# Retention in 64-token blocks on quarters of the TensorE array, with the key rotation, one DMA pair and two weight loads moved

## Chip, cores and metric

One NeuronCore of one Trainium2 chip runs the whole kernel. The metric is the device time in microseconds of one execution; a time of a kernel is the median of its runs. The profile is one such execution, and its times count from the first instruction (the span).

## What is computed

The reference is one layer of a streaming encoder for a prompt of 4096 tokens and a sample of 64 tokens, with model width 1024, all in fp32:

```python
h = _rmsnorm(x, norm_g) * (1.0 + scale) + shift
rq, rk, rv, rg, aq, ak, av, ag = _in_proj(h, w_in)      # one matmul, columns split
rq = _rope(rq, pos); rk = _rope(rk, pos) * RET_DK ** -0.5
r_out, state = _retention(rq, rk, rv)                   # 4 heads of 128
r_out = _head_norm(r_out) * jax.nn.silu(rg)
a_out = sliding_window_attention_with_sinks(aq, ak, av) * jax.nn.silu(ag)
x = x + gate * (concatenate([r_out, a_out]) @ w_out)
y = _rmsnorm(x, final_g)

def _retention_chunk(R, q, k, v):                       # one block of L tokens
    s = einsum('bqhd,bkhd->bhqk', q, k) * decay         # decay[i, j] = g**(i - j), 0 above the diagonal
    out = einsum('bhqk,bkhv->bqhv', s, v) + einsum('bqhd,bhdv->bqhv', q, R) * g**(i + 1)
    R = g**L * R + einsum('bkhd,bkhv->bhdv', k * g**(L - 1 - j), v)
```

The block length L is free as far as the result goes. The reference uses 64.

## The kernel before

Tokens go in tiles of 128: 32 tiles of the prompt (t = 0 to 31) and one (t = 32) that holds the sample in its upper half. The program has two phases, each a loop over tiles, and every engine has its own instruction list with waits on semaphores. SP issues all DMAs, in the order of its list.

Phase A (`slot`, t = 0 to 33) makes the four retention projections of tile t and the retention of tile t-1. The projections are split matmuls: activations and weights are each cut into a high and a low fp32r part, and three products of 8 matmuls of 512 columns are added (`dense`, L1298, the matmul itself L1305), so 24 matmuls for each of the groups q, k, v and gate. TensorE's order in a slot is: q projection into bank `za0`; the retention block of the tile before; k projection into `za1`; v into `za0`; gate into `za1`. A bank is written again only when VectorE or ScalarE have read it (`zq_read`, `zk_read`, `v_done`, `rg_done`).

The retention block (L1384 to L1404) is plain fp32 and works on the whole tile of 128 tokens: per head a 128x128 score matmul (L1389), a state update `k_row` x `v_dec` (L1395), and two matmuls into the bank `out_b`, the queries on the state (L1401) and the decayed scores on the values (L1403).

VectorE's list in a slot (L949 to L1057): transpose the keys (L958), scale the next tile's x (L913), decay the scores (L964), rotate the queries out of `za0` (L942, L944, L947), group norm statistics of `out_b` (L983), state update (L992), aggregate (L996), transpose the next tile's x (`turn_x`, L919), normalise `out_b` into `r_out` (L1005) and gate it (L1010), rotate the keys out of `za1` (L942 to L947 again), transpose and scale the queries (L1024, L1026), split the next tile's h into its parts (`split_h`, L926 and L928), decay the values (L1041), finish the gate (L1047). ScalarE modulates x into h between `turn_x` and `split_h` (L726), copies the values (L762) and takes the tanh of the gate (L774). GpSimd takes the powers for the two norms.

SP's list in a slot: store the scaled x (L445) and load it back in blocks of 32 rows for the transpose (L430), the same for the rotated queries (L461), store h (L469), load the next rope table (L471), store the retention output (L477), then the store and four loads of the rotated keys (L481, L430). The weights of the attention projections and of the output come in pieces of 1 MB through four staging buffers (`load_piece`, L290), are rounded by ScalarE (`split_hi`, L317) and their low part made by VectorE (`split_lo`, L321). At slot 4 TensorE also computes the output gate of adaLN (L1458), VectorE adds its bias (L1056), and SP stores it and then loads two weight pieces (L493 to L499).

Phase B (`slot_b`) does the attention and the output projection. Its matmuls for the attention use parts of the array: L1501 is stationary 128x64 (half the columns), L1508 is 64x64 (a quarter), L1478 is 64x128 (half the rows). A `tile_position` gives the rows and columns of the array.

Of the kernel before, what the change touches and what calls it, by code (L numbers as in the profile page):

```python
# [31 lines left out]
F32 = mybir.dt.float32  # L32
# [27 lines left out]
def build_program(nc, x_prompt, x_sample, c_prompt, c_sample, state_ret, cache_k, cache_v, norm_g, w_ada,  # L60
# [5 lines left out]
    with ctx:  # L66
# [14 lines left out]
        small = sb("small", [P, 64])  # L81
# [32 lines left out]
        decay = sb("decay", [P, COLS], F32, phase_a)  # L114
        qdec = sb("qdec", [P, COLS], F32, phase_a)
        tiny_a = sb("tiny_a", [P, 176], F32, phase_a)
# [3 lines left out]
        c_in = tiny_a[:, 36:52].rearrange("p (c k) -> p c k", c=2)  # L120
        c_th = tiny_a[:, 52:68].rearrange("p (c k) -> p c k", c=2)
        c_silu = tiny_a[:, 68:84].rearrange("p (k c) -> p k c", c=2)
        g_col = tiny_a[:, 84:92]
        h_scale = tiny_a[:, 108:124].rearrange("p (k c) -> p k c", c=2)
        h_shift = tiny_a[:, 124:140].rearrange("p (k c) -> p k c", c=2)
# [76 lines left out]
        state_out, wide_set = sem("state_out"), sem("wide_set")  # L202
# [182 lines left out]
        def ag_bank(i, t):  # L385

            return out0_b if static(i) and t == 0 else kg_b

        def static(i):
            return isinstance(i, int)  # L390

# [7 lines left out]
        def _(sp):  # L399
# [34 lines left out]
            def slot(i, u):  # L434
# [43 lines left out]
                if not pe_turns(i, t) and (not static(i) or t < SAMPLE):  # L478

                    wait(sp, k_done, t + 1)  # L480
                    sp.dma_start(k_dram[t], k_row[:, :]).then_inc(k_stored, 16)  # L481
                    wait(sp, k_stored, 16 * t)
                    wait(sp, x_turned, t)
                    load_blocks(k_in, k_dram[t], k_loaded)
# [8 lines left out]
                if static(i) and t == 4:  # L493
                    sp.wait_ge(gate_rows, 1)
# [3 lines left out]
                    for n in range(B_KV, B_Q + 1):  # L498
                        load_piece(sp, n)  # L499
# [398 lines left out]
        def _(dve):  # L898
# [50 lines left out]
            def slot(i, u):  # L949
# [11 lines left out]
                if back:  # L961
                    wait(dve, s_ready, t)
                    wait(dve, out_ready, t - 1)
                    V.tensor_tensor(s_t[:, :], qs_b[:, :], decay[:, :], ALU.mult).then_inc(st_done, 1)  # L964
                if front:
# [4 lines left out]
                    rotate(t, za0, q_row, zq_read, q_mul, q_done)  # L970
                if static(i) and t == SAMPLE:
# [7 lines left out]
                if back:  # L979
                    wait(dve, out_ready, t)  # L980
                    wait(dve, gn_mv_done, t - 1)
                    for h in range(RH):
                        last = V.bn_stats(gn_stats[:, h, :], out_b[:, h * DK:(h + 1) * DK])  # L983
# [4 lines left out]
                    wait(dve, upd_ready, t)  # L988
                    st = state_s if static(i) and t - 1 == SAMPLE else state
                    for h in range(RH):  # L990
                        cols = slice(h * DK, (h + 1) * DK)
                        last = V.scalar_tensor_tensor(st[:, cols], st[:, cols], GAMMA[h] ** P, upd_b[:, cols], ALU.mult, ALU.add)  # L992
# [5 lines left out]
                if more and not (static(i) and t == 0):  # L998
                    turn_x(*nxt)
                if back:  # L1000
                    wait(dve, gn_rstd_done, t)
                    wait(dve, yr_stored, 16 * (t - 1))
                    for h in range(RH):
                        cols = slice(h * DK, (h + 1) * DK)
                        last = V.tensor_scalar(r_out[:, cols], out_b[:, cols], gn_mv[:, h, 0:1], gn_rstd[:, h:h + 1],  # L1005
# [616 lines left out]
```

## Time and profile before

| | |
|---|---|
| median of 3 runs | 1841.93 us (1838.59 to 1841.97) |
| profiled execution | 1841.76 us |
| its span | 1840.0 us |
| TensorE matmul busy | 97% of the span |
| VectorE, ScalarE, GpSimd busy | 63%, 31%, 6% |
| mean granted TensorE clock | 0.991 |
| DMA | 296.64 MB, 161 GB/s over the span |

Phase A ends and phase B begins at about 886 us. An engine's busy share is an average over both phases and over the start and the change of phase; which engine sets the time has to be read in each. In a timeline row the first number is the start, the second the time from the start of the row's first instruction to the end of its last; the ends of matmuls are modelled, so the distance of starts is the better measure.

### The profile page before, as it was taken

What the parts mean: (1) busy time and instruction counts of PE and PEld (TensorE: products, weight loads), DVE (VectorE), ACT (ScalarE), POOL (GpSimd) and SP (SyncE); (2) the same over time, 40 slices, a digit from 0 to 9 for tenths busy, and PEclk for the clock granted to TensorE, in tenths of its full rate; (3) what the DMA queues carried; (4) which work ended last, traced back from release to release, by engine and by line L of the source; (5) the groups of instructions that cost most, each with busy time, mean ns of one, the idle gap of its engine ahead of it and who ended that gap; (6) DMA issues with size and microseconds to landing.
All of it is one profiled execution on the core that took longest, in us unless ns stands there. A gap on an engine that the chain in (4) does not pass through costs nothing.

```text
span 1840.0 us, 31120 instructions
## 1 busy us (share of the span) xinstructions
PE 1790.7 (97%) x9668; PEld 1482.1 (81%) x9668; DVE 1159.3 (63%) x2590; ACT 579.2 (31%) x2032; POOL 116.7 (6%) x278
## 2 busy tenths in 40 slices
PE   5999999999999999999799999999999999999997
PEld 2788788888888888888678888888888888888885
DVE  3665666655666555666756766766666666666666
ACT  3321222212222212222434434434434344344342
POOL 1000000000000000000000000000000000000000
PEclk8999999999999999999899999999999999999999
DMA  9666555555555554554666565575565665665655
GB/s 372 200 170 181 143 130 148 137 137 140 129 148 147 126 146 133 134 141 132 200 172 163 150 190 148 157 190 143 160 187 142 170 172 146 182 166 145 188 145 139
DMA packets 488481, 296.64 MB, mean 161 GB/s; under 512 B 348634, under 2 KB 423594, under 8 KB 487412
## 3 DMA queue, kind: packets, MB, share of 16 engines
q1 hardware_dynamic: 488436, 296.08, 58.5%
q8 instruction: 24, 0.39, 0.1%
q14 instruction: 21, 0.17, 0.0%
HBM read 174.27 MB, written 121.71 MB: 161 GB/s over the span
## 4 chain that ended last, share of the span: by engine, by line
PE 89%; issue 3%; DVE 3%; DMA 2%; SPq 1%; ACT 1%; POOL 0%; POOLq 0%; DVEq 0%; ACTq 0%
PE bank L1305 78%; PE bank L1478 3%; PE bank L1501 2%; PE bank L1403 2%; PE bank L1401 2%; PE bank L1395 2%; PE bank L1389 2%; PE bank L1508 1%; DVE wl L321 1%; DMA xn_scratch<-xn 1%; DMA xp<-xn_scratch 0%; DMA stage<-in_w_out 0%; SPq L517 0%; SPq L430 0%; DMA xt<-in_x_prompt 0%
## 5 line engine op out<-in xcount | busy, mean ns | idle before, releaser
L1305 PE MATMUL bank<-wh,hh 128*128 128x512 f32 x1584 | 399.6, 394 | 7.5 <-DVE hh L1085 2.7
L1305 PE MATMUL bank<-wl,hh 128*128 128x512 f32 x1584 | 391.9, 389 | 0.6 <-DVE wl L321 0.6
L1305 PE MATMUL bank<-wh,hl 128*128 128x512 f32 x1584 | 392.5, 390 | 0.0
L1305 PEld LDWEIGHTS bank<-wh,hh 128*128 128x128 f32 x1584 | 293.6, 189 | 69.0 <-issue 8.0
L1305 PEld LDWEIGHTS bank<-wl,hh 128*128 128x128 f32 x1584 | 297.5, 188 | 62.9 <-DVE wl L321 1.1
L1305 PEld LDWEIGHTS bank<-wh,hl 128*128 128x128 f32 x1584 | 297.9, 188 | 61.9
L726 ACT ACTIVATE hf<-xn,tiny_a 128x128 f32<-128x128 f32 (+1 forms) x248 | 98.6, 480 | 368.2 <-DVE xn L919 368.2
L1228 DVE SCALAR_TENSOR_TENSOR a_gate<-a_gate,bank 128x128 f32<-128x128 f32 x132 | 29.1, 282 | 174.9 <-ACT a_gate L875 174.9
L1305 PE MATMUL bank<-wh,yh 128*128 128x512 f32 x528 | 132.7, 393 | 0.0
L1305 PE MATMUL bank<-wh,yl 128*128 128x512 f32 x528 | 130.9, 389 | 0.0
L1305 PE MATMUL bank<-wl,yh 128*128 128x512 f32 x528 | 130.8, 389 | 0.0
L802 ACT ACTIVATE p_in<-bank,tiny_b 128x128 f32<-128x128 f32 x264 | 108.3, 410 | 33.6 <-DVE tiny_b L1123 33.6
L1305 PEld LDWEIGHTS bank<-wh,yh 128*128 128x128 f32 x528 | 100.0, 190 | 21.3 <-DVE yl L1159 0.4
L1305 PEld LDWEIGHTS bank<-wl,yh 128*128 128x128 f32 x528 | 99.3, 188 | 20.7
L1305 PEld LDWEIGHTS bank<-wh,yl 128*128 128x128 f32 x528 | 99.0, 188 | 20.7
L1047 DVE SCALAR_TENSOR_TENSOR r_gate<-r_gate,bank 128x512 f32<-128x512 f32 x33 | 22.7, 688 | 134.9 <-ACT r_gate L774 134.9
L805 ACT ACTIVATE p_in<-bank,tiny_b 128x64 f32<-128x64 f32 x264 | 95.4, 361 | 0.0
L964 DVE TENSOR_TENSOR s_t<-bank,decay 128x512 f32<-128x512 f32 x33 | 22.8, 692 | 97.3 <-PE bank L1389 97.3
L1117 DVE TENSOR_REDUCE tiny_b<-bank 128x2 f32<-128x384 f32 x132 | 67.7, 553 | 5.3
L875 ACT ACTIVATE a_gate<-bank 128x256 f32<-128x256 f32 x66 | 21.7, 381 | 156.2 <-PE bank L1305 156.2
L762 ACT ACTIVATE v_row<-bank 128x512 f32<-128x512 f32 x33 | 19.8, 599 | 153.8 <-DVE v_dec L1041 153.8
L805 ACT ACTIVATION_READ_ACCUMULATOR p_in<-bank,tiny_b 128x1 f32 x264 | 67.4, 255 | 0.0
(167 smaller groups left out, 2430.0 us busy)
## 6 DMA issues: line engine op xcount, KB each, us to landing
xt<-in_x_prompt SPq DMA_DIRECT2D x64, 512.0 KB, 4.0
p_scratch<-p_in SPq DMA_DIRECT2D x264, 96.0 KB, 1.8
p_in<-p_scratch SPq DMA_DIRECT2D x66, 384.0 KB, 3.4
h_scratch<-hf SPq DMA_DIRECT2D x33, 512.0 KB, 2.9
hf<-h_scratch SPq DMA_DIRECT2D x33, 512.0 KB, 4.9
out<-xt SPq DMA_DIRECT2D x32, 512.0 KB, 4.4
xn_scratch<-xn SPq DMA_DIRECT2D x31, 512.0 KB, 2.9
xp<-xn_scratch SPq DMA_DIRECT2D x124, 128.0 KB, 3.0
```

The source lines that it names most:

```text
L726: last = nc.scalar.activation(hf[:, k, lo:P], src, ACT.Identity, bias=h_shift[:, k, c:c + 1], scale=h_scale[:, k, c:c + 1])
L802: nc.scalar.activation(p_out[:, :, g, 2 * c, :], scores_g[:, whole:whole + P].rearrange("p (b c) -> p b c", b=4), ACT.Exp, bias=s_bias[:, ...
L805: nc.scalar.activation(p_out[:, 2 * c:2 * c + 2, g, 1, :], scores_g[:, part:part + HALF].rearrange("p (b c) -> p b c", b=2), ACT.Exp, bias ...
L1117: last = V.tensor_reduce(s_max[:, m:m + 2], s_banks[2 * half + g][:, 0:6 * HALF].rearrange("p (c k) -> p c k", c=2), mybir.AxisListType.X, ...
L1228: last = V.scalar_tensor_tensor(ag, ag, 1.0, z, ALU.add, ALU.mult)
L1305: ins = mm(out, a[:, k, :], b[:, k, :], start=first and n == part[0] and k == chunks[0], stop=last and n == part[-1] and k == chunks[-1])
L1389: last = mm(qs_b[:, c], k_t[:, c], q_t[:, c], start=True, stop=True)
L1395: last = mm(upd_b[:, c], k_row[:, c], v_dec[:, c], start=True, stop=True)
L1401: mm(out_b[:, c], q_t[:, c], st[:, c], start=True, stop=False)
L1403: last = mm(out_b[:, c], s_t[:, c], v_row[:, c], start=False, stop=True)
L1478: last = mm(s_banks[2 * half + g][:, c * 3 * HALF:(c + 1) * 3 * HALF], q[rows, 2 * half + c, :], window(k, rows, u, c), start=n == 0, stop ...
L1501: mm(weighed(i, t, c)[cols, :], v[:, cols], p_t[:, :, g, 2 * c, :], start=True, stop=False, tile_position=(0, g * HD))
```

## The change

The retention works in blocks of 64 tokens: two per tile, c = 0 and c = 1, on parts of the array that do not overlap.

- The scores of the two blocks are two matmuls of 64 moving columns per head, on the two column halves of the array. The cross part of the 128x128 scores is not computed.
- The state update of each block is a matmul over 64 rows, on the two row halves, into two banks (`upd_b`, `ky_b`). VectorE makes a state after the first block, `state_mid`, in addition to the state after the second.
- The queries of block 0 meet `state`, those of block 1 `state_mid`, on the two column halves; the decayed scores of 64x64 meet the values on quarters of the array. The odd heads put block 0 in the lower and block 1 in the upper rows of the output bank, and go to `xb0` instead of `out_b`.
- The matmuls that make the output (`weighted_values`) come behind the k projection in TensorE's list. In the last slot, which has no projection, they follow the update at once.
- VectorE rotates the keys, and transposes the next x, ahead of the group norm. It normalises and gates the output behind the split of h, at the slot's end. Odd heads are normalised in two halves.
- SP stores and loads the rotated keys ahead of the store of h, the rope load and the store of the output.
- At slot 4 SP loads one of the two weight pieces before it waits for the gate's rows; the rows and the other piece come at slot 5.

```diff
+        state_mid = sb("state_mid", [P, COLS], F32, phase_a)
@@ SP, slot(i, u)
+                if not pe_turns(i, t) and (not static(i) or t < SAMPLE):
+                    wait(sp, k_done, t + 1)
+                    sp.dma_start(k_dram[t], k_row[:, :]).then_inc(k_stored, 16)
+                    wait(sp, k_stored, 16 * t)
+                    wait(sp, x_turned, t)
+                    load_blocks(k_in, k_dram[t], k_loaded)
                 if not static(i) or t + 1 <= SAMPLE:
                     wait(sp, h_done, t + 2)
...
                     wait(sp, yr_done, t)
                     sp.dma_start(yr_dram[t - 1], r_out[:, :]).then_inc(yr_stored, 16)
-                if not pe_turns(i, t) and (not static(i) or t < SAMPLE):
...
                 if static(i) and t == 4:
+                    load_piece(sp, B_Q)
+                if static(i) and t == 5:
                     sp.wait_ge(gate_rows, 1)
...
-                    for n in range(B_KV, B_Q + 1):
-                        load_piece(sp, n)
+                    load_piece(sp, B_KV)
@@ VectorE, slot(i, u)
-                    V.tensor_tensor(s_t[:, :], qs_b[:, :], decay[:, :], ALU.mult).then_inc(st_done, 1)
+                    V.tensor_tensor(s_t[:, 0:RH * HALF], qs_b[:, 0:RH * HALF], decay[:, :], ALU.mult).then_inc(st_done, 1)
                 if front:
...
                     rotate(t, za0, q_row, zq_read, q_mul, q_done)
+                if back:
+                    wait(dve, upd_ready, t)
+                    wait(dve, out_ready, t - 1)
+                    wait(dve, state_done, t - 1)
+                    for h in range(RH):
+                        last = V.scalar_tensor_tensor(state_mid[:, cols], st[:, cols], GAMMA[h] ** HALF, upd_b[:, cols],
+                                                      ALU.mult, ALU.add)
+                    last.then_inc(mid_done, 1)
...
+                if front:
+                    wait(dve, za_ready, 4 * t + 2)
+                    rotate(t, za1, k_row, zk_read, k_mul, k_done)
+                if more and not (static(i) and t == 0):
+                    turn_x(*nxt)
+                if back:
+                    wait(dve, out_ready, t)
+                        last = V.bn_stats(gn_stats[:, h, :], out_of(h))
+                        last = V.scalar_tensor_tensor(st[:, cols], state_mid[:, cols], GAMMA[h] ** HALF, ky_b[:, cols],
+                                                      ALU.mult, ALU.add)
+                    last.then_inc(state_done, 1)
+                        last = V.bn_aggr(gn_mv[:, h, :], gn_stats[:, h, :])
...
                     V.tensor_tensor(heads(v_dec[:, :]), heads(za0[:, :]), vdec..., ALU.mult).then_inc(vdec_done, 1)
+                if more:
+                    split_h(*nxt)
+                if back:
+                    wait(dve, gn_rstd_done, t)
+                        if row_block(h, 0) == 0:
+                            last = V.tensor_scalar(r_out[:, cols], out_of(h), ...)
+                        else:
+                            for c in range(2):
+                                last = V.tensor_scalar(r_out[c * HALF:(c + 1) * HALF, cols], out_of(h)[at, :], ...)
+                    V.scalar_tensor_tensor(r_out[:, :], r_out[:, :], 0.5, r_gate[:, :], ALU.mult, ALU.mult).then_inc(yr_done, 1)
+                if front:
                     if static(i) and t == SAMPLE:
                         for n in range(B_GATE, B_OUT):
                             split_lo(dve, n)
@@ TensorE
+            def weighted_values(i, t):
+                wait(pe, gn_done, t - 1)
+                wait(pe, mid_done, t)
+                for h in range(RH):
+                    for c in range(2):
+                        cols, at = slice(h * DK, (h + 1) * DK), row_block(h, c)    # row_block: HALF * ((c + h) % 2)
+                        if h == RH - 1 and c == 1:
+                            wait(pe, st_done, t)
+                        mm(out_of(h)[at:at + HALF, :], q_t[:, h * DK + c * HALF:h * DK + (c + 1) * HALF],
+                           (st, state_mid)[c][:, cols], start=h < 2, stop=False, tile_position=(0, at))
+                for h in range(RH):
+                    for c in range(2):
+                        last = mm(out_of(h)[at:at + HALF, :], s_t[rows, h * HALF:(h + 1) * HALF], v_row[rows, cols],
+                                  start=False, stop=h >= 2, tile_position=(c * HALF, at))
+                last.then_inc(out_ready, 1)
...
                     for h in range(RH):
-                        last = mm(qs_b[:, c], k_t[:, c], q_t[:, c], start=True, stop=True)
+                        for c in range(2):
+                            last = mm(qs_b[c * HALF:(c + 1) * HALF, h * HALF:(h + 1) * HALF], k_t[:, tok], q_t[:, tok],
+                                      start=True, stop=True, tile_position=(0, c * HALF))
...
-                        last = mm(upd_b[:, c], k_row[:, c], v_dec[:, c], start=True, stop=True)
+                        for c in range(2):
+                            last = mm((upd_b, ky_b)[c][:, cols], k_row[rows, cols], v_dec[rows, cols], start=True, stop=True,
+                                      tile_position=(c * HALF, 0))
                     last.then_inc(upd_ready, 1)
-                    for h in range(RH):
-                        mm(out_b[:, c], q_t[:, c], st[:, c], start=True, stop=False)
-                        last = mm(out_b[:, c], s_t[:, c], v_row[:, c], start=False, stop=True)
+                    if not front:
+                        weighted_values(i, t)
...
                         dense(za1[:, :], h_hi, h_lo, group(1)).then_inc(za_ready, 1)
+                    if back:
+                        weighted_values(i, t)
```

Smaller edits follow from these: the gate's rows of slot 4 go to the free half of `qs_b`, one bank of phase B's first tile is another one, and the decay tables are made for 64 tokens.

## Rows read from the trace of the kernel before

**Rows 1.** The page: the chain that ended last, by engine.

```profile
PE 89%; issue 3%; DVE 3%; DMA 2%; SPq 1%; ACT 1%; POOL 0%; POOLq 0%; DVEq 0%; ACTq 0%
```

**Rows 2.** Timeline of TensorE over one slot of phase A (start, duration, instruction).

```profile
535.19 2.07 PE L1305 MATMUL bank<-wh,hh 128*128 128x512 f32 x8
537.11 1.98 PE L1305 MATMUL bank<-wl,hh 128*128 128x512 f32 x8
...
555.24 1.98 PE L1305 MATMUL bank<-wh,hl 128*128 128x512 f32 x8
557.05 1.05 PE L1389 MATMUL bank<-q_t,k_t 128*128 128x128 f32 x8
...
560.54 2.07 PE L1305 MATMUL bank<-wh,hh 128*128 128x512 f32 x8
```

**Rows 3.** Slot of phase A: length; PE, PEld, DVE, ACT, POOL busy; clock; DMA.

```profile
532.50:557.80 25.30, 25.30 (x130) 21.55 (x129) 15.63 (x33) 5.43 (x12) 1.96 (x4) 1.00 0.53 136
```

**Rows 4.** Timeline of TensorE over the attention of one slot of phase B.

```profile
1128.94 1.98 PE L1305 MATMUL bank<-wh,yl 128*128 128x512 f32 x8
1130.85 0.65 PE L1501 MATMUL bank<-s_row,v_prev 128*64 128x256 f32 x4
...
1131.86 0.43 PE L1508 MATMUL bank<-s_row,v_row 64*64 64x256 f32 x1
...
1132.13 0.38 PE L1508 MATMUL bank<-s_row,v_row 64*64 64x256 f32 x1
...
1132.46 0.36 PE L1478 MATMUL bank<-ak_h,aq_h 64*128 64x192 f32 x2
1132.65 0.27 PE L1478 MATMUL bank<-ak_l,aq_h 64*128 64x192 f32 x2
...
1133.76 0.28 PE L1478 MATMUL bank<-ak_h,aq_l 64*128 64x192 f32 x2
1133.97 1.22 PE L1305 MATMUL bank<-wkvh,hh 128*128 128x256 f32 x8
1135.03 1.12 PE L1305 MATMUL bank<-wkvl,hh 128*128 128x256 f32 x8
1135.99 1.12 PE L1305 MATMUL bank<-wkvh,hl 128*128 128x256 f32 x8
```

**Rows 5.** Timeline of VectorE and ScalarE over the same slot.

```profile
536.40 0.88 DVE L992 SCALAR_TENSOR_TENSOR state<-state,bank 128x128 f32<-128x128 f32 x4
...
538.43 1.25 DVE L919 STREAM_TRANSPOSE xn<-xp 128x1024 f32<-128x1024 f32 x1 [0.85 <-DMA xp<-xn_scratch]
539.60 1.33 DVE L1005 TENSOR_SCALAR r_out<-bank,tiny_a,small 128x128 f32<-128x128 f32 x4
...
539.85 3.19 ACT L726 ACTIVATE hf<-xn,tiny_a 128x128 f32<-128x128 f32 x8 [11.75 <-DVE xn L919]
```

**Rows 6.** Slot 5: the chain's longest DMA, then timeline rows of VectorE and TensorE.

```profile
170.97 8.49 DMA xn_scratch<-xn
...
185.12 1.25 DVE L919 STREAM_TRANSPOSE xn<-xp 128x1024 f32<-128x1024 f32 x1 [6.84 <-DMA xp<-xn_scratch]
...
172.41 1.05 PE L1389 MATMUL bank<-q_t,k_t 128*128 128x128 f32 x8
...
189.59 3.63 PE L1305 MATMUL bank<-wh,hh 128*128 128x512 f32 x8 [2.56 <-DVE k_row L944]
...
202.20 1.05 PE L1389 MATMUL bank<-q_t,k_t 128*128 128x128 f32 x8
```

**Rows 7.** Slot 1: timeline of TensorE at its first projection.

```profile
61.65 2.08 PE L1305 MATMUL bank<-wh,hh 128*128 128x512 f32 x8 [0.77 <-ACT v_row L762]
```

**Rows 8.** Slots 32 and 33: timeline of VectorE, then of TensorE.

```profile
878.54 4.48 DVE L321 TENSOR_TENSOR wl<-stage,wh 128x2048 fp32r<-128x2048 f32 x2
883.57 0.69 DVE L1047 SCALAR_TENSOR_TENSOR r_gate<-r_gate,bank 128x512 f32<-128x512 f32 x1 [0.55 <-ACT r_gate L774]
...
884.52 0.39 PE L1401 MATMUL bank<-state_s,q_t 128*128 128x128 f32 x2
```

More of the change, by code:

```diff
@@ L80, in build_program @@
         ident = sb("ident", [P, P])
-        small = sb("small", [P, 64])
+        small = sb("small", [P, 32])
         neg_half = small[:, 0:8]
@@ L385, in ag_bank, with row_block, out_of @@
         def ag_bank(i, t):
-            return out0_b if static(i) and t == 0 else kg_b
+            return out1_b if static(i) and t == 0 else kg_b
         def static(i):
             return isinstance(i, int)
+        def row_block(h, c):
+            return HALF * ((c + h) % 2)
+        def out_of(h):
+            return (out_b, xb0)[h % 2][:, h * DK:(h + 1) * DK]
         def pe_turns(i, t):
@@ L978, in slot @@
                         split_lo(dve, n)
-                if back:
-                    wait(dve, out_ready, t)
-                    wait(dve, gn_mv_done, t - 1)
-                    for h in range(RH):
-                        last = V.bn_stats(gn_stats[:, h, :], out_b[:, h * DK:(h + 1) * DK])
-                    last.then_inc(gn_stat_done, 1)
-                    wait(dve, gn_stat_done, t)
-                    wait(dve, gn_var_done, t - 1)
[L988 to L992, printed above, removed]
-                    last.then_inc(state_done, 1)
-                    for h in range(RH):
-                        last = V.bn_aggr(gn_mv[:, h, :], gn_stats[:, h, :])
-                    last.then_inc(gn_mv_done, 1)
[L998 to L1005, printed above, removed]
-                                               ALU.subtract, ALU.mult)
-                    last.then_inc(gn_done, 1)
-                    wait(dve, gn_done, t)
-                    wait(dve, rg_done, t)
-                    V.scalar_tensor_tensor(r_out[:, :], r_out[:, :], 0.5, r_gate[:, :], ALU.mult, ALU.mult).then_inc(yr_done, 1)
                 if front:
@@ L1031, in slot @@
                     split_lo(dve, B_KV)
-                if more:
-                    split_h(*nxt)
                 if static(i) and t == 0:
@@ L1366, in dense_kv @@
                 dense(kg_b[:, 0:KV], *h_of(i, t), (wkvh, wkvl)).then_inc(zb_ready, 1)
+            def weighted_values(i, t):
+                wait(pe, gn_done, t - 1)
+                wait(pe, mid_done, t)
+                st = state_s if static(i) and t - 1 == SAMPLE else state
+                for h in range(RH):
+                    for c in range(2):
[4 more added lines that the diff above has]
+                           (st, state_mid)[c][:, cols], start=h < 2, stop=False, tile_position=(0, at))
+                for h in range(RH):
+                    for c in range(2):
+                        rows, cols = slice(c * HALF, (c + 1) * HALF), slice(h * DK, (h + 1) * DK)
+                        at = row_block(h, c)
+                        last = mm(out_of(h)[at:at + HALF, :], s_t[rows, h * HALF:(h + 1) * HALF], v_row[rows, cols],
+                                  start=False, stop=h >= 2, tile_position=(c * HALF, at))
+                last.then_inc(out_ready, 1)
             def slot(i, u):
@@ L1443, in slot @@
                         wait(pe, k_done, t + 1)
+                        wait(pe, state_done, t)
                         for h in range(RH):
@@ L1486, in weigh @@
                 t = 2 * i + u
+                if static(i) and t == 0:
+                    pe.wait_ge(gn_done, SAMPLE + 1)
                 if static(i) and t == SAMPLE:
```

65 lines of the change are left out of this document (38 added, 27 removed).

## The prediction

> **What bounds the kernel now.** I read the page's chain first: 89% of it is TensorE [rows 1]. Then the timeline of TensorE in one slot of phase A. The distance between the first projections of two slots is 25.35 us (535.19 to 560.54). Ten rows of 8 projection matmuls take 18.13 us (537.11 to 555.24), 1.813 us a row, so the twelve rows of a slot take 21.76 us and 3.59 us are left for the retention block. The scores begin at 557.05, exactly one row after 555.24 [rows 2]. So in a steady slot TensorE never waits, and the block's 3.59 us are on the path in each of the 33 slots that have one. The block has 16 fp32 matmuls, recorded as two passes each: 32 passes of 128 columns, 0.112 us each. VectorE is busy 15.63 of 25.3 us of such a slot [rows 3]. Nothing but TensorE's own time, and the places where it does wait, can move the result.
>
> **The retention block.** After the change it has 32 matmuls, 64 passes, and all run on parts of the array. Phase B already works so, and its timeline gives both sides of the trade [rows 4].
>
> The gain: on quarters (L1508) four passes start together, at 1131.86 and again at 1132.13. On row halves (L1478) a pair starts every 0.111 us (1132.65 to 1133.76 is ten steps). On column halves (L1501) 8 passes of 256 columns take 1.01 us to the start of L1508; one after the other they would take 8 x 0.22 = 1.8 us, at 0.112 us for 128 columns. So halves do run two at a time and quarters four.
>
> The cost: each change of shape. Without one, the row at 1128.94 would end at 1130.75; L1501 begins at 1130.85, a gap of 0.10. L1501 needs 4 x 0.22 = 0.88 of its 1.01 us, so its own slow first step and the gap to L1508 cost 0.13 together. L1508's first step is 0.27 instead of 0.22, and L1478 comes 0.33 after the second, a gap of 0.11. L1478's first step is 0.19 instead of 0.11. From its last pair to the full array are 0.21 instead of 0.11, and the first full row takes 1.06 us (1133.97 to 1135.03) where the next takes 0.96. By kind: into column halves or quarters 0.10 + 0.05 = 0.15 us, into row halves 0.11 + 0.08 = 0.19, back to the full array 0.10 + 0.10 = 0.20.
>
> The sum for the new block, in its order:
> - Scores on column halves: 16 passes of 64 columns, 8 steps. No row has so short a pass. If time goes with columns it is 0.056 a step, 0.45 us; if a step has a floor at what the pairs of L1478 need, 0.111, it is 0.89 us. I take 0.46: on row halves the floor was there with 128 stationary columns, and here both operands have 64.
> - Update on row halves: 16 passes of 128 columns, 8 steps, 0.89 us.
> - Queries on the states, column halves: 8 steps, 0.89 us.
> - Scores on values, quarters: 4 steps, 0.45 us.
> - Six changes: into column halves 0.15, into row halves 0.19, to the full array 0.20 (the k projection), into column halves 0.15, into quarters 0.15, to the full array 0.20: 1.04 us. The update's first step may cost 0.11 instead of 0.08, as its passes are longer than those of L1478; I take 1.07.
>
> That is 2.69 + 1.07 = 3.76 us against 3.59: **0.17 us more in each slot**. What the array gains by packing (0.9 us) the six changes take back. Over the 32 slots that have projections: +5.4 us. Bounds: with the gaps alone (six of 0.10) the block is 3.29, 0.30 less; with the score floor and 0.22 for each change 4.44, 0.85 more: -9.6 to +27.2 us.
>
> The Trainium skill, TensorEngine Tiling (Array Packing), section Theoretical Speedup, allows up to 2x for one small dimension and up to 4x in 64x64 tiles. Taken alone it leaves the 2.69 us of streams and 29 us gained in 32 slots; the trace agrees with the factors, but not with that sum, because it shows the changes between them.
>
> **What hides the rest of a steady slot.** I lay the slot out from the q projection's start, with 1.81 us a row and 0.2 us from one engine to the next. TensorE: q to 5.4, scores and update to 7.3, k to 12.8, output matmuls to 14.4, v to 20, gate to 25.5.
> - VectorE's `state_mid` is four instructions like the state update, 0.88 us [rows 5]. It comes after the query rotation, from 8.8 to 9.7. TensorE needs it at 12.8: 3 us of cover. If that went, each microsecond over it would cost 32 us.
> - Two more half-size normalisations cost two of L1005's, 1.33 / 4 each, so 0.67 us [rows 5]; the score decay on half the columns saves at most 0.3. VectorE goes from 15.6 to about 16.9 of 25.5 us: nothing on the path.
> - Key rotation: 13.0 to 15.1 (from the k projection's end), read by the gate projection at 20: 5 us of cover. `turn_x` then takes 1.25 us to 16.3; before it stood at 12.2, and 0.85 us of that was a wait for its DMA [rows 5], which now has 3 us of room. ScalarE's modulation, 3.19 us [rows 5], ends at 19.6. `split_h` follows the v projection and `v_dec`, 21 to 22.8; the next q projection needs it at 25.5: 2.7 us of cover.
> - The output's normalisation and gate end at 25.5, the gate's end and the key transpose at 27.9, needed by the next scores at 30.9: 3 us.
> - SP: the key store and its four loads now come at 15 to 21, ahead of the h store (h ready at 19.6) and the rope load, which nobody needs before the next slot; the output's store is last, at 25.6, before the next slot's x store. GpSimd's power for the group norm is asked for at 18.4 and used at 22.8. Cost zero, by these covers.
>
> **Slot 5.** Before, two pieces of 1 MB go out ahead of slot 5's x store, which takes 8.49 us. `turn_x` waits 6.84 us for it, the key rotation stands behind `turn_x`, and TensorE stops at 189.59 and then runs its next 8 matmuls in 3.63 us, twice the usual. From scores to scores the slot takes 29.79 instead of 25.35 us (172.41 to 202.20) [rows 6]: 4.44 us lost. After, one piece is asked for before the x store and the key rotation no longer stands behind `turn_x`. Both would be enough: with a DMA as late as before `turn_x` ends 3 us later than planned and `split_h` still within the slot. **-4.4 us.** Bounds: 0 to -4.4.
>
> **Start.** At slot 1 TensorE waits 0.77 us for the copy of the values [rows 7], which waits for VectorE behind the split of h and the scaling of the sample's state. With `v_dec` ahead of the split the copy is hidden and the split ends last: -0.5 us (0 to -0.8). At slot 30 the order costs about as much, 0.2, since the split of a weight piece now stands ahead of `v_dec` and of `split_h` with it.
>
> **Slots 32 and 33.** Here VectorE is the late one. Before, it normalises the output of slot 32 while TensorE works, splits two weight pieces from 878.54 for 4.48 us, finishes the gate at 883.57, and slot 33's output matmuls start at 884.52 [rows 8]. Now the normalisation (1.33 + 0.67) and its gate (0.69, an instruction like L1047) stand behind `v_dec`, ahead of the weight pieces: 2.7 us in the queue that were hidden before, less about 1 us in which VectorE waited for the v projection. Then come the gate's end, the score decay, and 0.88 us of `state_mid`, for which slot 33's output matmuls wait with nothing else to do. They start about 2.4 us later. What follows in phase B's start hangs on TensorE and on VectorE's next weight pieces, so it moves along: **+2.4 us** (0 to 3.5). Phase B itself is as before.
>
> **Sum.** +5.4 - 4.4 - 0.5 + 0.2 + 2.4 = +3.1 us on the profiled execution's 1841.76 us, 0.17 below the median: about **1845 us**.
>
> **Rivals.**
> - *The changes of shape are mostly hidden* (faster). If the weight load of the new shape overlaps the last passes of the old, the gaps alone are left and the block is 3.29: 1841.8 - 9.6 - 2.3 = 1830 us. For it: nothing in the old block shows a gap. Against it: all four changes in phase B show gap and slow first step in one sum. It decides once the six changes cost less than 0.85 us (block under 3.55, at which the total is 0.2% under). Chance 0.18.
> - *Short passes have a floor, or the passes of odd and even heads do not pair.* Scores at 0.111 a step: +0.43 a slot, 14 us more, 1859. In `weighted_values` the halves follow as A B B A, where phase B has A B A B; if each second pair went one after the other the state part would take 1.34 instead of 0.89, again 14 us. Against it: two passes per matmul already pair across halves. Chance 0.2.
> - *Slot 5 keeps its stall*, the pieces at slots 4 and 5 each delaying an x store: 1849. Chance 0.08.
> - The forecast as summed: 0.54.
>
> **Numbers.** A difference of 0.2%, 3.7 us, is about what a measurement of this kernel can tell from none. The forecast's own range, 1840 to 1850, crosses the upper bound of that (1845.6): of its 0.54 some 0.34 are within 0.2% and 0.2 slower. With the rivals: faster 0.18, same 0.34, slower 0.48. The 80% range reaches half way to the fast rival and nearly to the floor: 1835 to 1858.
>
> **What would show it.** Per slot: scores to scores 25.5 us, six short gaps in TensorE, scores row under 0.6 us, no wait of TensorE for `state_mid`. Slot 5 as long as slot 6. Slot 33: TensorE waits for `state_mid` for 2 us. I am wrong if the distance of slots is under 25.3 (changes cheaper) or over 25.8 (floor or broken pairs), or if TensorE waits for VectorE in steady slots.

## The result and the profile after

The kernel after takes **1864.55 us** (median of 4 runs, 1863.7 to 1866.37), the kernel before 1841.76. The ratio is 1.0128, interval 1.0116 to 1.014: slower by 1.3%. The forecast was 1845, its range 1835 to 1858; the result lies above the range. The profiled execution took 1863.72 us with a span of 1861.6, so it is 21.65 us longer than the span before, of 1839.96.

The chain on the page, by engine, says that the bound is still TensorE [rows 1]:

```profile
PE 91%; issue 3%; DVE 2%; DMA 2%; ACT 1%; POOL 1%; SPq 0%; POOLq 0%; DVEq 0%; ACTq 0%
```

The timeline of TensorE over one slot of phase A, after (start, duration, instruction), answers to [rows 2]:

```profile
534.54 0.69 PE L1438 MATMUL bank<-q_t,k_t 128*64 128x64 f32 x16
535.16 1.16 PE L1446 MATMUL bank<-v_dec,k_row 64*128 64x128 f32 x16
536.25 2.13 PE L1333 MATMUL bank<-wh,hh 128*128 128x512 f32 x8
538.22 2.02 PE L1333 MATMUL bank<-wl,hh 128*128 128x512 f32 x8
540.08 2.02 PE L1333 MATMUL bank<-wh,hl 128*128 128x512 f32 x8
542.03 0.32 PE L1406 MATMUL bank<-state,q_t 128*64 128x128 f32 x1
...
543.06 0.67 PE L1412 MATMUL bank<-v_row,s_t 64*64 64x128 f32 x16
543.65 2.13 PE L1333 MATMUL bank<-wh,hh 128*128 128x512 f32 x8
545.62 2.02 PE L1333 MATMUL bank<-wl,hh 128*128 128x512 f32 x8
547.48 2.02 PE L1333 MATMUL bank<-wh,hl 128*128 128x512 f32 x8
...
556.75 1.98 PE L1333 MATMUL bank<-wl,hh 128*128 128x512 f32 x8
558.56 1.98 PE L1333 MATMUL bank<-wh,hl 128*128 128x512 f32 x8
560.47 0.69 PE L1438 MATMUL bank<-q_t,k_t 128*64 128x64 f32 x16
```

The block stands in two pieces, as planned, and TensorE never waits. But look at the projections, whose code the change doesn't touch. From 538.22 to 540.08 and from 545.62 to 547.48 a row of 8 takes 1.86 us, where [rows 2] have 1.81. The rows from 556.75 on take 1.81. The first nine rows of this slot multiply `hh1` and `hl1`, the last three, the next tile's queries, `hh0` and `hl0`. So slots alternate: 25.93 us with nine rows of `hh1` and `hl1`, 25.71 with three; the mean is 25.82, against 25.35 before.

Phase B, which the change leaves alone but for banks, has the same. The timeline of its output projection after, and a slot of phase A and one of phase B in the windows view (length; PE, PEld, DVE, ACT, POOL busy; clock; DMA):

```profile
1134.91 2.03 PE L1333 MATMUL bank<-wh,yh 128*128 128x512 f32 x8
1136.78 2.02 PE L1333 MATMUL bank<-wl,yh 128*128 128x512 f32 x8
1138.64 2.02 PE L1333 MATMUL bank<-wh,yl 128*128 128x512 f32 x8
...
534.54:560.47 25.93, 25.93 (x162) 20.71 (x161) 17.20 (x39) 5.43 (x12) 1.96 (x4) 1.00 0.52 134
1120.00:1148.26 28.26, 28.26 (x164) 22.94 (x164) 18.20 (x46) 11.07 (x50) 1.34 (x5) 1.00 0.57 162
```

Rows on `yh` and `yl` take 1.86 us too. Before they took 1.81: this row starts so much ahead of the first one of [rows 4], at 1128.94:

```profile
1127.13 1.98 PE L1305 MATMUL bank<-wl,yh 128*128 128x512 f32 x8
```

Rows on `hh0` stay at 1.81; a slot of phase B takes 28.26 instead of 27.98 us. The granted clock is 1.00, the upper of its two levels (2.4 GHz), in the slots of both phases, as in [rows 3], so the clock is not the cause.

The other places that the prediction named, after: slot 1's first projection, the scores of slots 5 and 6, then TensorE's waits at slots 31 and 33 and what VectorE does ahead of the second (in brackets the idle time before an instruction and what ended it):

```profile
60.31 2.13 PE L1333 MATMUL bank<-wh,hh 128*128 128x512 f32 x8
...
173.09 0.69 PE L1438 MATMUL bank<-q_t,k_t 128*64 128x64 f32 x16
198.99 0.69 PE L1438 MATMUL bank<-q_t,k_t 128*64 128x64 f32 x16
...
866.52 2.12 PE L1333 MATMUL bank<-wh,hh 128*128 128x512 f32 x8 [0.92 <-DVE hl L938]
...
897.54 0.29 PE L1406 MATMUL bank<-state_s,q_t 128*64 128x128 f32 x1 [2.55 <-DVE state_mid L988]
...
891.19 4.49 DVE L322 TENSOR_TENSOR wl<-stage,wh 128x2048 fp32r<-128x2048 f32 x2
```

The wait of slot 1 [rows 7] is gone. Slot 5 takes 25.90 us, as its neighbours do, where [rows 6] have 29.79. At slot 33 the state matmuls wait 2.55 us for `state_mid`, behind two weight splits: the wait that was forecast. At the end of slot 31 there is a wait for the split of h that was not.

### The profile page after: what moved, and what is told of

It is laid out like the page before. It is cut to its first block, busy times and chain, and to the rows that moved or that the text cites. A ratio compares the mean times of both kernels' runs of the same rounds, so it can differ in the third digit from the quotient of the medians.

```text
span 1861.6 us, 33496 instructions
## 1 busy us (share of the span) xinstructions
PE 1814.7 (97%) x10724; PEld 1452.6 (78%) x10724; DVE 1209.7 (65%) x2788; ACT 579.4 (31%) x2032; POOL 116.1 (6%) x278
## 4 chain that ended last, share of the span: by engine, by line
PE 91%; issue 3%; DVE 2%; DMA 2%; ACT 1%; POOL 1%; SPq 0%; POOLq 0%; DVEq 0%; ACTq 0%
PE bank L1333 80%; PE bank L1527 3%; PE bank L1446 2%; PE bank L1552 2%; PE bank L1406 2%; PE bank L1438 1%; PE bank L1559 1%; PE bank L1412 1%; DVE wl L322 1%; DMA stage<-in_w_in 0%; DMA stage<-in_w_out 0%; DMA xn_scratch<-xn 0%; SPq L439 0%; ACT wh L318 0%; POOL small L654 0%
## 5 line engine op out<-in xcount | busy, mean ns | idle before, releaser
L1333 PE MATMUL bank<-wh,hh 128*128 128x512 f32 x1584 | 406.5, 398 | 5.3 <-DVE hh L1113 2.7
L952 DVE TENSOR_TENSOR bank<-bank,rope 128x512 f32<-128x512 f32 x66 | 45.8, 694 | 111.7 <-PE bank L1333 111.7
L815 ACT ACTIVATION_READ_ACCUMULATOR p_in<-bank,tiny_b 128x1 f32 x264 | 67.3, 255 | 0.0
L812 ACT ACTIVATION_READ_ACCUMULATOR p_in<-bank,tiny_b 128x1 f32 x264 | 65.5, 248 | 0.0
L697 POOL TENSOR_TENSOR v_prev<-v_row,small 128x128 f32<-128x128 f32 x31 | 12.4, 401 | 844.5 <-PE bank L1559 844.5
```

Of the source, the lines that this page charges most:

```text
L812: nc.scalar.activation(p_out[:, :, g, 2 * c, :], scores_g[:, whole:whole + P].rearrange("p (b c) -> p b c", b=4), ACT.Exp, bias=s_bias[:, ...
L815: nc.scalar.activation(p_out[:, 2 * c:2 * c + 2, g, 1, :], scores_g[:, part:part + HALF].rearrange("p (b c) -> p b c", b=2), ACT.Exp, bias ...
L952: V.tensor_tensor(swap[:, :].rearrange("p (h e d) -> p h e d", h=RH, e=2), z4[:, :, ::-1, :], sin, ALU.mult).then_inc(mul, 1)
L1333: ins = mm(out, a[:, k, :], b[:, k, :], start=first and n == part[0] and k == chunks[0], stop=last and n == part[-1] and k == chunks[-1])
```

## The experiments

All runs are variants of the kernel before (labels with b_, and best) or after (a_, a64_). Each time is a median, with the ratio to the kernel before on the same chip and its interval. The runs were spread over several chips, on which the kernel before took 1840.1 to 1841.8 us, so the ratios compare better than the times. "Slot" is the distance from scores to scores on TensorE.

### One line of the diff alone

The slow rows share one thing: their stationary tiles are allocated behind `small`, which the change cut from 64 to 32 columns; the diff printed above does not show that line. `hh0` and `hl0` lie ahead of it.

**b_small32:** the kernel before with that one line of the change.

```
-        small = sb("small", [P, 64])
+        small = sb("small", [P, 32])
```

> The kernel before with one edit of the change alone: the tensor small has 32 columns instead of 64 (the columns above 27 are unused), so every SBUF tensor allocated after it starts 128 bytes lower in each partition. Address theory (the start of the stationary tiles hh1, hl1, yh and yl is what lengthens the projection matmuls): rows of 8 on the odd tiles of phase A take 1.86 us instead of 1.81, slots of phase B 28.26 instead of 27.98, and the time is about 16*12*0.047 + 33*0.28 = 18 us longer, 1860. Rival (the longer rows come from the new retention code, the array changes or the longer program): no change, 1842.

1858.42 us, ratio 1.0098 (1.0083 to 1.0114). Phase B's slot takes 28.26 us, phase A's 25.85 and 25.51 by turns. One line that computes nothing costs 17 of the 22.8 us.

**a_small64:** the kernel after with that line undone.

```
-        small = sb("small", [P, 32])
+        small = sb("small", [P, 64])
...
-        tiny_a = sb("tiny_a", [P, 96], F32, phase_a)
-        vdec = tiny_a[:, 0:4]
...
+        tiny_a = sb("tiny_a", [P, 88], F32, phase_a)
+        vdec = small[:, 32:36]
...
```

> The kernel after with small at 64 columns again (four constants moved into it and tiny_a shortened, so that the rest fits). Address theory: every row of 8 takes 1.81 us again, the mean slot of phase A about 25.54 and of phase B 27.98 us, time 1845 to 1847, within 0.3% of the kernel before. Rival (the retention code or the array changes lengthen the rows): 1864 as after.

1849.44 us, 1.0041 (1.0028 to 1.0055). Its slot on TensorE:

```profile
530.85 0.69 PE L1438 MATMUL bank<-q_t,k_t 128*64 128x64 f32 x16
...
534.51 1.99 PE L1333 MATMUL bank<-wl,hh 128*128 128x512 f32 x8
536.33 1.97 PE L1333 MATMUL bank<-wh,hl 128*128 128x512 f32 x8
...
556.40 0.69 PE L1438 MATMUL bank<-q_t,k_t 128*64 128x64 f32 x16
```

Rows of 1.81 again, every steady slot 25.56 us, phase B's 27.98. The retention change without the shift costs +0.21 us a slot and, with its ends, 8 us; the time is above what was expected by 2.4, which the runs on slot 31 below explain.

**b_tiles128 and b_s32_pad:** which of the tensors that moved it is. The first changes the offset of the four stationary tiles alone (what follows them moves by whole multiples of 512 bytes); the second moves the staging buffers and what stands ahead of `yh` in phase B, and leaves the four where they were.

```
+        pad_a = sb("pad_a", [P, 32], F32, phase_a)
         hh1 = sb("hh1", [P, KC, P], F32R, phase_a)
...
+        pad_b = sb("pad_b", [P, 32])
         yh = sb("yh", [P, KC, P], F32R)
```

b_tiles128 has these two lines and 384 bytes behind `hl1` and `yl`; b_s32_pad has them and `small` at 32 columns.

> The kernel before with small unchanged, but 128 bytes of padding right ahead of hh1 and of yh, and 384 bytes right behind hl1 and yl: only hh1, hl1, yh and yl change their offset, by 128 bytes; all other tensors keep theirs to a multiple of 512. Address theory with the stationary tiles as the cause: as b_small32, about 1860. Rival (another tensor that moved is the cause, such as the moving k and v weights or the staging buffers): 1842.

> The kernel before with small at 32 columns, and 128 bytes of padding right ahead of hh1 and of yh: the stationary tiles (and what follows them) stand where they stood, while the staging buffers, the k and v weights of phase B and phase B's other tensors ahead of yh stand 128 bytes lower. Address theory with the stationary tiles as the cause: 1842. Rival (tensors ahead of them): 1860.

1859.34 us, 1.0105 (1.0089 to 1.012), and 1838.71, 0.9988 (0.9978 to 0.9997). Two rows on `yh` and `yl` of b_tiles128, then of b_s32_pad:

```profile
1129.29 2.03 PE L1309 MATMUL bank<-wh,yh 128*128 128x512 f32 x8
1131.16 2.02 PE L1309 MATMUL bank<-wl,yh 128*128 128x512 f32 x8
```

```profile
1120.37 1.98 PE L1307 MATMUL bank<-wh,yh 128*128 128x512 f32 x8
1122.18 1.98 PE L1307 MATMUL bank<-wl,yh 128*128 128x512 f32 x8
```

1.87 against 1.81 us from row to row. It is the start of the stationary tile itself; moving the staging buffers and phase B's other tensors costs nothing (slots of phase B even get a little shorter, which the last section follows up).

### Which starts cost

Six more sizes of `small` in the kernel before, nothing else changed: 48 and 80 columns with 10 and 4 runs, 128, 112, 72 and 40 with a single run each.

> The kernel before with small at 48 columns: hh1, hl1, yh and yl start 192 bytes behind a multiple of 512 instead of 256. If only a start 128 bytes from a multiple of 256 costs, 1842; if any start that is not a multiple of 256 costs the same, 1859; if a start that is no multiple of 128 costs more, above 1860.

> The kernel before with small at 80 columns: hh1, hl1, yh and yl start 64 bytes above a multiple of 256 (with 48 columns it was 64 below, and the pair of slots cost 0.25 us more, against 0.66 at 128). If the cost goes with the distance from a multiple of 256: 1842 to 1844. If a start above is worse than one below: up to 1859.

> The kernel before with small at 128 columns: the stationary tiles start at a multiple of 512 bytes. Control: if multiples of 256 are free, rows of 8 with yh take 1.813 us and the time is 1840 to 1842; if the free offset is 256 behind a multiple of 512 alone, 1.86 and 1859.

> The kernel before with small at 112 columns: the tiles start 448 bytes behind a multiple of 512, 64 below the next one. If 64 below a multiple of 256 is cheap, as with 192: rows of 1.83 us, 1843. If only 192 is: 1.86, 1857 to 1859.

> The kernel before with small at 72 columns: the tiles start 32 bytes above 256. If every start above a multiple costs in full: rows of 1.86 us, 1857 to 1859. If the cost goes with the distance: less than at 64 above, 1850 or under.

> The kernel before with small at 40 columns: the tiles start 160 bytes behind a multiple of 512, 96 below 256. If the cost falls from 128 to 192 step by step: rows between 1.832 and 1.858 us, 1845 to 1855. If it is a step function of 64 bytes: 1.858 as at 128.

Start of the tiles behind a multiple of 512 bytes, counted by the sizes of the tensors ahead of them from the kernel's first tensor (no view shows the address on the chip); a row of 8 on `yh` or `yl` (from the first to the last of six successive rows, by five); the time:

| start | row, us | time, us | kernel |
|---|---|---|---|
| 0 | 1.81 | 1837.43 (one run) | b_small128 |
| 256 | 1.81 | 1841.8 | before |
| 192 | 1.83 | 1843.14, ratio 1.0015 (1.0006 to 1.0024) | b_small48 |
| 448 | 1.83 | 1844.22 (one run) | b_small112 |
| 128 | 1.86 | 1858.42 | b_small32 |
| 384 | 1.86 | 1859.34 | b_tiles128 |
| 160 | 1.87 | 1860.18 (one run) | b_small40 |
| 288 | 1.87 | 1858.9 (one run) | b_small72 |
| 320 | 1.87 | 1857.16, ratio 1.0097 (1.0081 to 1.0112) | b_small80 |

The rows behind the two ends and the middle, of b_small128, b_small112 and b_small72:

```profile
1120.86 1.98 PE L1305 MATMUL bank<-wh,yh 128*128 128x512 f32 x8
1122.67 1.98 PE L1305 MATMUL bank<-wl,yh 128*128 128x512 f32 x8
```

```profile
1128.70 2.00 PE L1305 MATMUL bank<-wh,yh 128*128 128x512 f32 x8
1130.53 1.99 PE L1305 MATMUL bank<-wl,yh 128*128 128x512 f32 x8
```

```profile
1135.62 2.03 PE L1305 MATMUL bank<-wh,yh 128*128 128x512 f32 x8
1137.49 2.03 PE L1305 MATMUL bank<-wl,yh 128*128 128x512 f32 x8
```

What counts is the start's remainder by 256 bytes: 0 is free, 192 costs 0.02 us a row, and every other one tried (32, 64, 128, 160) costs 0.05 or a little more. The cost does not go with the distance, since 32 bytes above a multiple is as dear as 128. b_small128 ran 3.3 us under the one run of before on its chip. By the profiles it is 4.3 shorter: 2.15 of that were there by slot 6, from the start and from a shorter stall at slot 5 (28.20 us), and the rest came at slot 30 and at the start of phase B, so this one run says nothing on 0 against 256 beyond the equal rows.

### Slot 5: the pieces or the rotation

**b_pieces:** the spread of the weight pieces alone.

```
                 if static(i) and t == 4:
+                    load_piece(sp, B_Q)
+                if static(i) and t == 5:
                     sp.wait_ge(gate_rows, 1)
...
-                    for n in range(B_KV, B_Q + 1):
-                        load_piece(sp, n)
+                    load_piece(sp, B_KV)
```

> The kernel before with the weight pieces of slots 4 and 5 spread as in the change (one at slot 4, the stores and the other at slot 5), nothing else. Theory that either edit ends the stall of slot 5: scores of slot 5 to scores of slot 6 in 25.4 instead of 29.8 us, time 1841.8 - 4.4 = 1837.4. Rival that the order of VectorE is needed too: some part of the 4.4 us stays, at slot 5 or moved to slot 6.

1836.35 us, 0.9978 (0.9968 to 0.9987). The scores of slots 5 and 6:

```profile
171.90 1.05 PE L1390 MATMUL bank<-q_t,k_t 128*128 128x128 f32 x8
197.24 1.05 PE L1390 MATMUL bank<-q_t,k_t 128*128 128x128 f32 x8
```

25.34 us: the whole stall is gone.

**b_rot:** the key rotation ahead of `turn_x` on VectorE alone. **b_rot_sp:** the same, with the key store ahead of the h store on SP.

```
+                if front:
+                    wait(dve, za_ready, 4 * t + 2)
...
+                    rotate(t, za1, k_row, zk_read, k_mul, k_done)
                 if more and not (static(i) and t == 0):
                     turn_x(*nxt)
...
```

> The kernel before with the key rotation ahead of turn_x on VectorE, nothing else: both pieces still go out at slot 4. Theory that either edit ends the stall of slot 5: turn_x is as late as before, but the gate projection no longer waits for it, so slot 5 takes 25.4 to 26 us, time 1837.4 to 1838. Rival: the wait moves to the split of h, and 2 us or more of the 4.4 stay.

> The kernel before with the key rotation ahead of turn_x on VectorE (as b_rot) and, as in the change, the key store and its loads ahead of the h store on SP; both pieces still at slot 4. In b_rot TensorE waited some 0.35 us ahead of the scores of every steady slot for the turned keys, which waited 3.5 us for their loads, asked for behind the h store. Theory that SP's order is the missing link: steady slots of 25.35 us again, slot 5 under 26 us, 1837 to 1838. Rival (the later turn_x itself is too late for the split of h): slots stay at 25.8, about 1860.

1860.41 us, 1.0111 (1.0096 to 1.0127), and 1844.97, 1.0023 (1.0013 to 1.0033). In a steady slot of b_rot, the scores on TensorE and the turned keys that they wait for:

```profile
538.98 1.13 PE L1390 MATMUL bank<-q_t,k_t 128*128 128x128 f32 x8 [0.28 <-DVE k_t L958]
...
538.12 0.71 DVE L958 STREAM_TRANSPOSE k_t<-xp 128x512 f32<-128x512 f32 x1 [3.50 <-DMA xp<-k_scratch]
```

A later `turn_x` makes h later, and SP waits with the h store: it goes out 15.9 us behind the scores, 11.4 before. The key store queues behind it (17.7 instead of 13.1), the keys come late, and steady slots rise to about 25.9 us. With the key store first (b_rot_sp) they are back at 25.35. Neither run mends slot 5, though. In b_rot_sp, scores, TensorE's wait and VectorE's queue there:

```profile
172.45 1.05 PE L1390 MATMUL bank<-q_t,k_t 128*128 128x128 f32 x8
195.17 2.48 PE L1306 MATMUL bank<-wh,hh 128*128 128x512 f32 x8 [2.65 <-ACT v_row L762]
202.36 1.05 PE L1390 MATMUL bank<-q_t,k_t 128*128 128x128 f32 x8
...
190.50 0.71 DVE L1025 STREAM_TRANSPOSE q_t<-q_row 128x512 f32<-128x512 f32 x1 [2.13 <-DMA q_row<-q_scratch]
191.85 0.69 DVE L926 CAST hh<-hf 128x1024 fp32r<-128x1024 f32 x1
```

29.91 us: the keys no longer wait, but the split of h and `v_dec` stand behind the turning of the queries, whose store and loads stand behind the late x loads on SP. The stall has moved to the next projection.

Both runs also have a stall that the kernel before lacks. Slot 30 takes 30.21 us in b_rot_sp and 30.27 in b_rot, where before it takes 25.88. VectorE and TensorE there, in b_rot_sp:

```profile
828.21 2.29 DVE L321 TENSOR_TENSOR wkvl<-stage,wkvh 128x2048 fp32r<-128x2048 f32 x1 [1.74 <-ACT wkvh L317]
833.74 2.71 PE L1306 MATMUL bank<-wh,hh 128*128 128x512 f32 x8 [2.99 <-ACT v_row L762]
```

A weight piece is rounded by ScalarE behind its modulation of x, and split by VectorE ahead of the split of h and `v_dec`; with `turn_x` later, all of that comes later, and the copy of the values last. These 4.3 us are most of the 4.9 by which b_rot_sp is above before on its chip.

### The last slots of phase A

**a64_piece31:** a_small64 with the last weight piece asked for one slot later. **a64_both:** this, and the two splits for the gate weights behind `state_mid` of slot 33.

```
-                if static(i) and t == NT - 2:
+                if static(i) and t == NT - 1:
                     load_piece(sp, B_Q + 1)
...
                 if static(i) and t == SAMPLE + 1:
+                    for n in range(B_GATE, B_OUT):
+                        split_lo(dve, n)
```

The last two added lines, with their removal from slot 32, are in a64_both alone.

> The kernel after with small at 64 columns (as a_small64), the last weight piece of phase A asked for at slot 31 instead of 30, and the two splits for the gate weights on VectorE moved from slot 32 to behind state_mid of slot 33. Theory: TensorE's gap at the end of slot 31 (3.2 us in a_small64) comes from that piece delaying the x store, and falls to 0.4; the gap of 2.8 us ahead of slot 33's state matmuls comes from the splits in VectorE's queue, and falls to 1 or less. With both, 1849.4 - 2.8 - 1.9 = 1844.7. Rivals: the gap of slot 31 stays (order of VectorE alone); the later splits lengthen the start of phase B by what slot 33 gains, 1846.6.

> The kernel after with small at 64 columns, and the last weight piece of phase A asked for at slot 31 instead of 30 (the half of a64_both that took the gap of slot 31 away; the splits for the gate weights stay at slot 32). Theory: slot 31 takes 25.6 us instead of 28.65, and phase B's start is as in a_small64: 1849.4 - 3.1 = 1846.3. Rival: the piece, later by a slot, is late for its split at slot 32, and phase B's start gives back up to 3 us: 1849.

1849.11 us, 1.0042 (1.0028 to 1.0055), and 1846.2, 1.0034 (1.0022 to 1.0045). In a_small64 the projection at the end of slot 31 waited 2.79 us for the split of h:

```profile
861.28 2.11 PE L1333 MATMUL bank<-wh,hh 128*128 128x512 f32 x8 [2.79 <-DVE hl L938]
```

In both new kernels that wait is gone; from slot 31 to 32 they take 25.56 (a64_both) and 25.85 us instead of 28.65. So the piece made it: its 1 MB is asked for 3 us ahead of the x store, which in a_small64 is out at 839.18 and read back from 846.41 on. In the kernel after the chain there runs from an x store of 6.01 us through the x loads and the queries' store and loads to the split of h. That is slot 5's mechanism again, at another slot. Phase B's first scores come 35.4 us behind those of slot 33 in a64_piece31, 33.7 in a_small64: some of the gain is given back there. By the profiles a64_piece31 is 3.0 us shorter than a_small64; by the runs the two are 6.1 and 8.0 us above before, each on its own chip, and their intervals overlap.

In a64_both the wait for `state_mid` fell too, but two others appeared:

```profile
887.35 0.29 PE L1405 MATMUL bank<-state_s,q_t 128*64 128x128 f32 x1 [1.07 <-DVE state_mid L988]
892.80 1.22 PE L1332 MATMUL bank<-wkvh,hh 128*128 128x256 f32 x8 [3.76 <-DVE hl L944]
...
923.12 0.53 PE L1526 MATMUL bank<-ak_h,aq_h 64*128 64x192 f32 x2 [9.93 <-DVE ak_l L1281]
```

Phase B's first scores come 38.6 us behind slot 33's. In this passage TensorE waits for VectorE each time, and what this move gained at one wait came back at the next two: phase B's first scores are 3.2 us further behind slot 33's than in a64_piece31, though the intervals of the two ratios overlap.

### The best version

**best:** b_pieces with the padding of b_s32_pad and its `small` of 32 columns.

> The kernel before with the spread pieces of b_pieces and the padding of b_s32_pad (stationary tiles where they were, phase B's tensors ahead of yh 128 bytes lower), in which slots of phase B took 27.93 instead of 27.98 us. If the two add up: 1836.3 - 30 x 0.05 = 1834.9 or less. Rival (the gain of b_s32_pad was all at slot 5 and at the start): 1836.

1834.6 us, 0.997 (0.9959 to 0.9982): faster than both kernels. By the profiles a slot of phase B takes 27.95 us, half of the gain hoped for there; another microsecond lies ahead of slot 1. Against b_pieces the intervals overlap.

## Why the prediction was wrong

In spans: +21.65 us, by the distances between scores. The start, the slots, slot 5 and the ends are read from the kernel after, and the split between block and rows from a_small64:

| step of the prediction | forecast | measured |
|---|---|---|
| retention block, per slot and in all | +0.17, +5.4 | +0.21, 31 distances: +6.6 |
| slot 5 | -4.4 | -4.4 |
| start | -0.5 | -1.1 |
| slot 30 | +0.2 | +0.2 |
| slot 31 | none | +1.2 |
| slots 32 and 33 | +2.4 | +2.5 |
| **projection rows, phase A** | none | 31 x 0.26 = **+8.0** |
| **phase B, "itself as before"** | none | **+8.7** |

**The step that failed** is the first: "twelve rows of a slot take 21.76 us", taken over for after, and with it "Phase B itself is as before". The diff was costed by the instructions that it moves; the line that shortens `small` issues none, is not in the diff as printed, and was costed at nothing without a word. It moves every later tensor by 128 bytes, and four of them are stationary operands of the projections: 16.7 of the 21.65 us. Without the two bold lines the sum is +4.9, 1846.7, and a_small64 at 1849.44 would have been inside the range.

**The block** was right to 0.04 us: 25.56 - 21.76 = 3.80 against 3.76. The rival of a floor for short passes falls: the 16 passes of the scores start at 534.54 and the update at 535.16, 0.62 us with a change of shape, where the floor alone needed 0.89. The rival of broken pairs falls: from the state part at 542.03 to the quarters at 543.06 are 1.03, not the 1.34 and more of unpaired steps. The rival of hidden changes falls: 3.80 less the 2.69 of the streams leaves 1.11 for the six changes, where 1.07 were taken from phase B's rows. The packing gains nothing here, because what it saves is paid for changes of shape.

**Slot 5** was right in size, wrong in why. "Both would be enough" holds for the pieces only (b_pieces). With the rotation alone the stall moves to the split of h (b_rot_sp); the forecast laid out `turn_x` and `split_h` but not the queries' store and loads, which SP issues behind the late x loads and VectorE waits for ahead of the split. The 4.4 us were also not the wait alone. [rows 6] give a wait of 2.56 us and 8 matmuls in 3.63 us; b_small128 has the same wait and the same 8 matmuls in 2.11. The windows view of those 8 matmuls in the kernel before, and the timeline of b_small128:

```profile
189.59:193.22 3.63, 3.63 (x9) 2.85 (x10) 3.36 (x5) 0.00 (x0) 0.00 (x0) 0.53 0.81 275
...
189.04 2.11 PE L1305 MATMUL bank<-wh,hh 128*128 128x512 f32 x8 [2.56 <-DVE k_row L944]
```

Behind the wait the granted clock of the kernel before fell to 0.53, nearly all of the stretch at the lower level (1.2 GHz); in b_small128 it stayed at 1.00 and slot 5 took 28.20 us. So about 1.6 of the 4.4 us are the clock, which fell after the same wait in one run and not in the other.

**Slot 31** is the same omission. The piece of slot 30 is still asked for about 3 us ahead of the next x store, as before; but that store now goes out 0.8 us behind the scores instead of 2.2 ahead of them, and the cover is used up. The trace shows why it is late: ScalarE's tanh of the gate waits 4.50 us for VectorE to normalise and gate the output, which now stands at the slot's end, and the squares for the next tile's norm stand behind the tanh. I costed that piece at slot 30 only.

**Slots 32 and 33 and the covers of a steady slot** came as written: the wait for `state_mid` is there, and TensorE waits for nothing in a steady slot, though VectorE is busy 17.20 us of one instead of 16.9. Slot 1 has lost its wait too, but the size of the start's gain is not shown: slot 1's scores come 1.1 us earlier than before in the kernel after, beyond the bound of 0.8, and 0.2 in a_small64; in b_s32_pad, which leaves the code of the start alone, they come 1.7 earlier.

## What to carry to other kernels

Read a change of a tensor's size as a change of the address of everything behind it, and check first whether rows that the change does not touch still have their duration; when they don't, undo the sizes before the algorithm. Put the stationary tiles of the costliest matmuls at a multiple of 256 bytes on purpose (counted here from the first tensor), with the odd-sized small tensors behind them, and then look at the rows again, since moving operands seem to have a preference of their own (next section). A big load that is spread out must be checked against the store that follows it at every slot where one is issued, and an instruction that is moved on one engine takes its DMA queue's order with it: b_rot lost 1.1% for want of that.

## What was not expected of the hardware

A fp32r matmul of 128x512 on a stationary tile that starts at a multiple of 256 bytes is issued every 0.227 us (1.81 / 8); 128 bytes off it is 0.232, 2.5% more, with the clock at 1.00 in both. The Trainium skill, SBUF — State Buffer, section Operand start alignment, lets a fp32 operand start at any multiple of 4 bytes and says that the rule is on legality and that its runs timed nothing; these runs show that legal starts differ in speed. What in the chip makes the difference stays open: the runs move the tile and see the step change, and nothing in them tells the load of the weights from the matmul itself.

Moving the tensors of phase B ahead of `yh` by 128 bytes gave slots shorter by 0.05 us (27.93 in b_s32_pad). The traces show where: in the rows on `wkvh` and `wkvl`, the moving operands of the attention's k and v projection, and in the row behind them. Their stationary tiles, `hh0` and `hl0`, lie ahead of `small` and never move. In b_small48, whose `wkvh` starts at 192:

```profile
1137.43 1.07 PE L1305 MATMUL bank<-wkvl,hh 128*128 128x256 f32 x8
1138.33 1.07 PE L1305 MATMUL bank<-wkvh,hl 128*128 128x256 f32 x8
```

A row of 8 takes 0.91 us here (the next row starts at 1139.24), and also in b_small80 and b_small112; in [rows 4], where `wkvh` starts at 256, it takes 0.96, and so it does in b_small128 and b_tiles128. At 32, 128 and 160 behind a multiple of 256 it takes 0.93 to 0.95. So for these moving operands a multiple of 256 is the slowest start tried, the other way round than for the stationary tiles. The three groups of rows take 2.84 instead of 2.98 us in b_small48; an estimate from that is 4.5 us over phase B's 32 tiles for a kernel that moves `wkvh` and `wkvl` alone, which no run tried. Other tensors moved with them in each of these runs, so the moving operand as the cause is read from the rows and not tested by itself.
